# Setup of the S5 matrices and rotations, an early small tile, another order of the first loads, and where mixer pieces may stand in a one-core hybrid encoder layer

## The reference, cut to what matters

```
h = RMSNorm(x); u = h @ W_in          # four groups of heads
x += concat(RG-LRU, Mamba-2 SSD, gated DeltaNet, S5) @ W_out
x += CrossAttn(RMSNorm(x), memory)    # 4 heads, 256 memory tokens
x += SwiGLU(RMSNorm(x)); final RMSNorm
```

```
step = exp(log_dt);  mag = exp(a_re*step);  ang = a_im*step
lb = mag*(cos ang + i sin ang);  f = (lb - 1)/a
bb_re = f_re*b_re - f_im*b_im;   bb_im = f_re*b_im + f_im*b_re
s_t = lb*s_(t-1) + bb @ u_t;     y = Re(C s) + D u
```

## Time and profile before

| what | us |
|---|---|
| median of 3 runs | 4091.99 (4088.88 to 4100.78) |
| the profiled execution, its device time | 4092.89 |
| its span, first to last instruction | 4091.1 |
| TensorE busy | 3659.4 (89%) |
| VectorE busy | 2256.5 (55%) |
| ScalarE busy | 1335.2 (33%) |
| GpSimd busy | 126.5 (3%) |
| mean granted TensorE clock | 0.942 |

### The profile page before, as it was taken

One profiled execution on the slowest core, in us unless ns is written; L12 is line 12 of the kernel. 1 busy time (PEld: TensorE's weight loads), 2 busy tenths in 40 slices (PEclk: granted clock), 3 DMA queues, 4 the chain that ended last, 5 costly groups with the idle time before them and its releaser, 6 DMA issues.

```text
span 4091.1 us, 63447 instructions
## 1 busy us (share of the span) xinstructions
PE 3659.4 (89%) x24122; PEld 3547.7 (87%) x24122; DVE 2256.5 (55%) x4638; ACT 1335.2 (33%) x2474; POOL 126.5 (3%) x354
## 2 busy tenths in 40 slices
PE   6777868889798999998899998899998899999998
PEld 5766768889788999988899998899997899998998
DVE  6656744377674766573645573555564556553323
ACT  5443332254533333432322332323232322322101
POOL 2400000000000000000000000000000000000000
PEclk8977977799898999999999999999999999999999
DMA  6654476577767677768566668456667556567776
GB/s 216 228 180 155 164 237 224 168 237 269 250 221 276 232 251 265 269 209 281 180 210 208 231 218 282 171 189 226 222 226 255 191 188 210 198 210 253 248 252 218
DMA packets 371566, 912.03 MB, mean 223 GB/s; under 512 B 34752, under 2 KB 174528, under 8 KB 370752
## 3 DMA queue, kind: packets, MB, share of 16 engines
q1 hardware_dynamic: 371264, 907.99, 64.3%
HBM read 733.28 MB, written 174.57 MB: 222 GB/s over the span
## 4 chain that ended last, share of the span: by engine, by line
PE 50%; issue 20%; DVE 13%; DMA 5%; ACT 4%; DVEq 3%; POOLq 2%; SPq 1%; POOL 1%; ACTq 1%; PEld 0%; PEldq 0%
PE banks L461 14%; PE banks L463 13%; PE banks L462 13%; DMA wlo_sb<-kept_dram 2%; DVE wlo_sb L1121 2%; DVE uc_sb L1212 2%; PE banks L1611 1%; PE banks L1605 1%; DVE m_p_sb L2178 1%; PE banks L877 1%; PE banks L1614 1%; DMA kept_dram<-wlo_sb 1%; ACT whi_sb L929 1%; DMA ldb_sb<-y_dram 1%; DVE m_p_sb L2148 1%
## 5 line engine op out<-in xcount | busy, mean ns | idle before, releaser
L461 PE MATMUL banks<-hh_sb,whi_sb 128*128 128x384 f32 (+1 forms) x3360 | 1153.1, 343 | 117.2 <-DMA wlo_sb<-kept_dram 27.4
L462 PE MATMUL banks<-hh_sb,wlo_sb 128*128 128x384 f32 (+1 forms) x3360 | 1122.3, 334 | 0.0
L463 PE MATMUL banks<-hl_sb,whi_sb 128*128 128x384 f32 (+1 forms) x3360 | 1121.2, 334 | 0.0
L461 PEld LDWEIGHTS banks<-hh_sb,whi_sb 128*128 128x128 f32 x3360 | 652.7, 194 | 145.4 <-issue 46.4
L462 PEld LDWEIGHTS banks<-hh_sb,wlo_sb 128*128 128x128 f32 x3360 | 653.7, 195 | 1.4 <-issue 0.3
L463 PEld LDWEIGHTS banks<-hl_sb,whi_sb 128*128 128x128 f32 x3360 | 652.0, 194 | 0.0
L461 PE MATMUL banks<-g_hi_sb,whi_sb 128*128 128x384 f32 (+2 forms) x1504 | 514.5, 342 | 73.2 <-DVE x_sb L1317 26.8
L463 PE MATMUL banks<-g_lo_sb,whi_sb 128*128 128x384 f32 (+2 forms) x1504 | 501.3, 333 | 0.0
L462 PE MATMUL banks<-g_hi_sb,wlo_sb 128*128 128x384 f32 (+2 forms) x1504 | 501.2, 333 | 0.0
L461 PEld LDWEIGHTS banks<-g_hi_sb,whi_sb 128*128 128x128 f32 x1504 | 295.5, 196 | 87.5 <-DVE x_sb L1317 30.1
L1317 DVE TENSOR_TENSOR x_sb<-x_sb,banks 128x384 f32<-128x384 f32 (+2 forms) x400 | 202.4, 515 | 281.1 <-PE banks L463 272.1
(11 more groups left out here) (433 smaller groups left out, 5235.2 us busy)
## 6 DMA issues: line engine op xcount, KB each, us to landing
whi_sb<-kept_dram SPq DMA_DIRECT2D x504, 512.0 KB, 3.8
wlo_sb<-kept_dram SPq DMA_DIRECT2D x504, 512.0 KB, 4.9
raw_sb<-w SPq DMA_DIRECT2D x176, 512.0 KB, 5.3
kept_dram<-whi_sb SPq DMA_DIRECT2D x112, 512.0 KB, 5.5
kept_dram<-wlo_sb SPq DMA_DIRECT2D x112, 512.0 KB, 6.4
uc_dram<-uc_sb SPq DMA_DIRECT2D x90, 192.0 KB, 2.8
ldb_sb<-x_t SPq DMA_DIRECT2D x72, 192.0 KB, 4.7
plain_sb<-w SPq DMA_DIRECT2D x32, 256.0 KB, 4.8
```

What stands on the lines that cost most here:

```text
L461: eng.matmul(out, xh, yh, start=first, stop=False)
L462: eng.matmul(out, xl, yh, start=False, stop=False)
L463: return eng.matmul(out, xh, yl, start=False, stop=last)
```

## The change

It has six parts (the wait for `tail_loaded` is now in `dve_unit` for pass 0, the last two hunks are of `dve_mixer` and of ScalarE's block). `z0` becomes the third entry of stage A of pass 0, right after the first `st`, and the memory tiles are then prepared in `z0, u9, u10, u11`. `may_follow` also forbids pieces before a `pt`. `s5b` holds only the 16 columns of each matrix; GpSimd multiplies over 128 elements, clears bb (2 x 2 x 640) at its start and writes the blocks into it, and no longer computes `rot` but for its first column. The doubling steps run on VectorE at setup pieces 6 to 12; the first of them waits for `setup_pool` 5, and `setup_rot` tells their end. The token scalars of pass 0 are done earlier: ScalarE's part (`act_gates`) at setup piece 12, VectorE's reciprocal at 14. The first weight and three token tiles are loaded ahead of the constants, and ScalarE does one small activation before it waits for `par`.

```diff
     a = stage_a(0, h, n)
+    a[2:2] = [a.pop(-2)]
     h, n = new_h("M", 0), new_norm("M", 0)
     spread(a[2:6], preps("M", 0, h, n))
...
-    return not (... or i + 1 < len(SECS) and SECS[i + 1].kind == "st")
+    return not (... or i + 1 < len(SECS) and SECS[i + 1].kind in ("st", "pt"))
...
-            s5b = sb(st, "s5b", [P, 2, 1024])
-            bb = sb(st, "bb", [P, 2, 8, P])
+            s5b = sb(st, "s5b", [P, 2, 128])
+            bb = sb(st, "bb", [P, 2, 2, 640])
...
+            eng.wait_ge(tail_loaded, 16)
...
+        def sp_constants(eng):
+            eng.dma_start(stail[:]..., t["conv_caches"]).then_inc(tail_loaded, 16)
+            for name, dst in (("s5p", ...), ("s5b", ...), ("smix", smix[:]), ("mixc", mixc[:])):
+                eng.dma_start(dst, t[name]).then_inc(const_loaded, 16)
             if i == 0:
-                sp_weights(eng, 0, RAWS)
-                sp_tiles(eng, s.preps)
+                sp_weights(eng, 0, 1)
+                sp_tiles(eng, s.preps[:LDS])
+                sp_weights(eng, 1, RAWS)
+                sp_constants(eng)
+                sp_tiles(eng, s.preps[LDS:])
...
                 elif n == 12:
+                    act_gates(eng, 0)
...
+            eng.memset(bb[:], 0.0)
             eng.wait_ge(const_loaded, 16 * 4)
...
+            eng.tensor_copy(rot[:, 0, :, 0], w_cos)
+            eng.tensor_copy(rot[:, 1, :, 0], w_sin)
+            parts = [v3(bt[:, 0, j * 128:j * 128 + 128], 8) for j in range(4)]
+            for dst, f, b in zip(parts, (fr, fi, fr, fi), (b_re, b_im, b_im, b_re)):
+                tt(dst, f, b, ALU.mult)
+            eng.drain()
+            for part, op in ((0, ALU.subtract), (1, ALU.add)):
+                for half in range(2):
+                    r = slice(half * 64, half * 64 + 64)
+                    for j in range(2):
+                        at = slice(4 * j, 4 * j + 4)
+                        out = v3(bb[r, part, j, :], 4)[:, :, half * 16:half * 16 + 16]
+                        tt(out, parts[2 * part][r, at, :], parts[2 * part + 1][r, at, :], op)
             eng.drain().then_inc(setup_pool, 1)
...
+        def dve_rotations(eng, n):
+            cn = rot[:, 0, :, n - 1:n].unsqueeze(1).to_broadcast([P, 2, 8, n])
+            sn = sin[:, :, n - 1:n].to_broadcast([P, 8, n])
+            tt(ta, sin[:, :, 0:n], sn, ALU.mult)
+            tt(tb, cos[:, :, 0:n], sn, ALU.mult)
+            tt(rot[:, :, :, n:2 * n], rot[:, :, :, 0:n], cn, ALU.mult)
+            eng.drain()
+            tt(cos[:, :, n:2 * n], cos[:, :, n:2 * n], ta, ALU.subtract)
+            tt(sin[:, :, n:2 * n], sin[:, :, n:2 * n], tb, ALU.add)
+            eng.drain()
...
+                elif 6 <= n < 13:
+                    if n == 6:
+                        eng.wait_ge(setup_pool, 5)
+                    dve_rotations(eng, 1 << n - 6)
+                    if n == 12:
+                        eng.drain().then_inc(setup_rot, 1)
+                elif n == N_SETUP - 2:
+                    dve_invert(eng, 0)
...
             act.wait_ge(begun, 1)
+            act.activation(rms[:, 0:1], eps[:], ACT.Square)
             act.wait_ge(par_loaded, 16)
```

More of the change, by code:

```diff
@@ L356 @@
     SQ_COUNT.update((x.ni, x.sq + 1) for x in _s.preps if x.sq >= 0)
-Q_END = [max(s.q + s.nf for s in SECS if s.kind == "z" and s.p == p) for p in range(NP)]
+Q_END = [max(s.q + s.nf for s in SECS if s.kind in ("u", "z") and s.p == p) for p in range(NP)]
 Q_KV = max(s.q + 2 for s in SECS if s.kind in ("fs", "fv"))
@@ L400, in may_follow @@
     s = SECS[i]
-    return not (s.kind == "w" and s.a == KD - 1 or i + 1 < len(SECS) and SECS[i + 1].kind == "st")
+    return not (s.kind == "w" and s.a == KD - 1 or i + 1 < len(SECS) and SECS[i + 1].kind in ("st", "pt"))
 CHUNK_SECTIONS, SAMPLE_SECTIONS, SCALAR_SECTIONS, N_SETUP = 21, 25, 4, 16
@@ L1458, in after_mixer @@
             return bool(s.preps) and s.preps[0].kind == "Y"
+        def sp_constants(eng):
+            eng.dma_start(stail[:].rearrange("p a b c -> p (a b c)"), t["conv_caches"]).then_inc(tail_loaded, 16)
+            for name, dst in (("s5p", s5p[:].rearrange("p a b -> p (a b)")), ("s5b", s5b[:].rearrange("p a b -> p (a b)")),
+                              ("smix", smix[:]), ("mixc", mixc[:])):
+                eng.dma_start(dst, t[name]).then_inc(const_loaded, 16)
         def sp_section(eng, i):
@@ L1863, in pe_mixer @@
                         for s in range(8):
-                            last = eng.transpose(banks[:, 3 + 2 * part + s // 4, s % 4 * P:s % 4 * P + P],
-                                                 bb[:, part, s, :], ident)
+                            at = slice(s % 4 * P, s % 4 * P + P)
+                            last = eng.transpose(banks[:, 3 + 2 * part + s // 4, at], bb[:, part, s // 4, at], ident)
                     last.then_inc(setup_pe, 1)
@@ L2024, in act_scalars @@
             eng.drain().then_inc(tok_act, 1)
+        def act_scalars(eng, p):
+            n = tiles(p)
+            if p:
+                act_gates(eng, p)
             yield
@@ L2586, in setup @@
[L2586 to L2590, removed]
-            eng.drain()
[L2592 to L2604, removed]
-                tt(sin[:, :, n:2 * n], sin[:, :, n:2 * n], tb, ALU.add)
-                eng.drain()
-                if n > 1:
-                    yield
-                n *= 2
+            eng.tensor_copy(rot[:, 0, :, 0], w_cos)
@@ L2611, in dve_mixer, with dve_invert @@
+        def dve_invert(eng, p):
+            eng.wait_ge(tok_den, p + 1)
+            z = tk[:, 5, 0:tiles(p) * 8]
+            eng.reciprocal(z, z).then_inc(tok_inv, 1)
         def dve_mixer(eng):
@@ L2620, in dve_mixer @@
                 yield
-                eng.wait_ge(tok_den, p + 1)
-                z = tk[:, 5, 0:tiles(p) * 8]
-                eng.reciprocal(z, z).then_inc(tok_inv, 1)
+                if p:
+                    dve_invert(eng, p)
                 yield
@@ L2762, in _ @@
             dve.wait_ge(par_loaded, 16)
-            dve.wait_ge(tail_loaded, 16)
             weave(dve, dve_section, dve_mixer)
@@ L2774, in _ @@
             sp.dma_start(par[:], t["par"]).then_inc(par_loaded, 16)
-            sp.dma_start(stail[:].rearrange("p a b c -> p (a b c)"), t["conv_caches"]).then_inc(tail_loaded, 16)
-            for name, dst in (("s5p", s5p[:].rearrange("p a b -> p (a b)")), ("s5b", s5b[:].rearrange("p a b -> p (a b)")),
-                              ("mixc", mixc[:]), ("smix", smix[:])):
-                sp.dma_start(dst, t[name]).then_inc(const_loaded, 16)
             weave(sp, sp_section, sp_mixer)
```

32 lines of the change are left out of this document (15 added, 17 removed).

## The result

The changed kernel takes 4062.9 us (median of four runs, 4053.9 to 4067.9), the kernel before, on the same chip, 4096.4 (4088.9 to 4101.0). The ratio is 0.9921, with a 95% interval from 0.9908 to 0.9933: by the ratio 32 us off, where 48 were forecast. The profiled execution of the changed kernel is its fastest, 4053.93 us with a span of 4052.1: it ends 39 us earlier than the profiled execution of before. So the trace shows 7 us more than the medians, and I use it for where time went, not for how much in all.

A forecast was written before the change was run, and what follows sets the result against it. TensorE bounds the kernel from 1100 us on, so gains lie in the first 250 us and repeated gaps of later passes. Terms -6 - 4 - 13 - 5 - 20 = -48 take 4092.0 to 4044; range 4030 to 4058.

The forecast's parts named there:

- sign of being wrong: The prediction is wrong if the set-up and turn stretches are shorter and the passes as long as before.
- First loads: Kernel start: first weight and token tiles ahead of constants bring the first section forward; -6 us (3 to 9).
- z0 early: Set-up: `z0` moves from a stage bound by TensorE to one that is not; -4 us (0 to 7).
- Scalars early: Around `k13`: TensorE's 11.65 us wait for GpSimd's sums and the slow clock after it go; -13 us (8 to 15).
- Narrow matrices and rotations: Set-up, 103 to 172 us: GpSimd's interference goes (-17.5), VectorE gets doubling steps (+4) and a wait (+8); -5 us net.
- No mixer before a turn: Passes 1 to 4, `s1` to `s3`: stalls before turns go, part returns in `vo`; -20 us (5 to 40).
- Slower: Replanning: each of 110 displaced pieces lands where TensorE must wait, losing 60 us; 4104 us, chance 0.05.
- The turns gain nothing: Passes: the stall before the turn returns in `vo` because VectorE is behind there; 4064 us, chance 0.17.
- VectorE binds the setup: Set-up: the wait for GpSimd and all rotations are exposed, early `z0` brings nothing; 4061 us, chance 0.11.

The follow-up runs named there:

- z0s_late: Changed kernel with `z0` back before `z1`'s place and pass 0's token scalars back where they were; ratio to the kernel before 0.9945 (0.9929 to 0.9961).
- wide: Changed kernel with the 1024-column S5 matrices and the doubling steps back on GpSimd; ratio to the kernel before 0.9943 (0.9923 to 0.9963).
- rot_pool: Changed kernel, narrow matrices kept, with only the doubling steps back on GpSimd; ratio to the kernel before 0.9921 (0.9906 to 0.9936).
- turn_only: Kernel before with only the new rule of no mixer piece in front of a turn; ratio 0.9972 (0.9961 to 0.9983), 11.5 us faster.
- shift: Kernel before with mixer pieces from pass 0's windows on spread half a piece earlier, turns keeping theirs; ratio 1.0005 (0.9992 to 1.0019).
- hybrid: `rot_pool` with only pieces ahead of turns moved (into `s3`, `vo`) in passes 0, 1, 4, the change's spreading in 2, 3; 4043.0 us, ratio 0.9867.
- rp_late: `rot_pool` with the old plan, except places ahead of turns moved behind `vo` to free `g`, `up` or `so` sections; ratio 0.9945 (0.9928 to 0.9962).

## Why the prediction was right, and where it was off

Its signs came: the first product at 11.4 us, no wait of TensorE for GpSimd near 230, L1209's taps at 352 ns, VectorE's wait for GpSimd (8.1 us, 10 forecast), 20.6 us from `s1` to `s3` (but for pass 4) with waits ended by ScalarE's drain, new waits for L1317 (L1320 now) in `vo`. In passes 1 and 4 its sign of being wrong came as well: the stretches are shorter and the passes as long as before (-0.2 and +2.2 us). The direction and most mechanisms were right, and the sum was 16 us too large: by the ratios some 8 in the set-up and 8 at the turns. That it came out this near is in part luck, since in two terms errors of opposite sign cancel.

- **First loads, 6 us.** 5.4 at `u8` in this trace, 3.8 to 5.4 in all eight with these loads; in `z0s_late`, where no `z0` is in between, 4.6 are left at `k5`. Tile 3 was worked out to come at 15.8 us and came at 15.6. Right, and a little large.
- **z0 early, 4 us.** 1.2, not told from nothing. Against `z0s_late` it costs 1.5 us by `k0`, less than the 2.5 paid in the working, but 3.1 by `fs3.0`; and of the 6.9 us where it stood only 4.7 come free, since `fs3.1` then waits. The term took the removal for full, and nearly all is paid back.
- **Scalars early, 13 us.** The jump is 15 us, and 4.7 come back in `fv1`: 10.6. The step that failed is "what is late next is nothing that I find": it looked at chunk 0's loads, and the late one was ScalarE's work in chunk 0's first piece, behind a wait of 3.64 us for a weight.
- **Narrow matrices and rotations, 5 us net.** By the places at `k11`, 12.6 less 4.6 of loads and 1.2 of `z0`: 6.8, to some 2 us. The net was near by errors that cancel. I took the whole excess of VectorE (15.5 us) and 2 of clock as gain; the runs give some 9, since part of the excess lay beside ScalarE's work: where it is gone, VectorE waits longer for ScalarE before its splits (10.1 us before 14 splits in `wide`, 17.4 before 17 in `rot_pool`). And I charged 12 us for the wait and the steps on VectorE; they cost 3 to 6. The 8.1 us wait is real, but wait and steps together cost less than its length.
- **No mixer before a turn, 20 us.** The working was 55.5 gross, 15 for TensorE work that moves, 20 for stalls in `vo`. Passes 1 to 4 show 51.2 gross: 14.2, 15.0, 13.8 and 8.2, for pass 4 does not get to 20.6 but to 24.9. `vo` gives back 14.9 in the four (4.3, 4.4, 4.3, 1.9), of which 9.6 are longer busy time of TensorE, so that 5 are left for stalls, not 20. From `vo0.3` to `w7` of the next pass another 22.1 go (9.7, 3.4, 0.4, 8.6). So 37 us come back where 35 were charged, but mostly elsewhere: the total is near because the stalls in `vo` were priced some 15 us too high and the rest of the pass too low. What is left is 14 us in this trace, and 11.5 by the ratio of `turn_only`; of the difference to 20, some 4 are pass 4's stretch. The step that failed is the last: "110 pieces of five windows move by a section or so; I cost that at nothing, since their number is the same". 110 is the number of places that move. The pieces run in one order, so 273 of the 401 run later than before, by one to six sections, and their number is not the same in each part of a pass: the FFN's second half gets 25 pieces in place of 23, with 44 more products, some 5 to 8 us of TensorE in passes 1 and 2.

The rival *Slower* had this mechanism, with a price on each displaced piece. `shift` shows that being displaced costs nothing on the whole; the table shows that a placement has a price of its own in each of passes 1 to 4, of either sign. The rival *The turns gain nothing* is nearest to the total, 4064, and right in that `vo` gives part back, but the turns do keep more than half of what I gave them. *VectorE binds the setup* falls: from 103 to 172 us TensorE does more work than before, and wait and steps cost 3 to 6 us.

What stays open: which sections of the FFN make pass 4 dear and passes 2 and 3 cheap, whether `vo` would be free without any piece, and why pass 0 differs by up to 12 us between executions of one plan.

## What to carry to other kernels

Where side work is woven into a main stream by a spreading rule, a new exclusion re-deals every piece behind it. Write down which piece runs in which place before and after, and not only where the places are; price the new places section by section, and read the gain from one recurring point of a pass to the next, where from pass 1 on it repeats to 3 us while whole runs scatter by 10 and more. Here the first two pieces of a chunk in a row were 5 to 6 us dearer than with a section between them. When a stall is removed, follow the stretch behind it to the end of the pass: here some 37 of 51 us came back, part as moved work and part as stalls elsewhere. A helper engine's interference is worth less than the stretched time that it causes, because part of that lies beside other waits; and an expected wait costs less than its length for the same reason.

## What the hardware showed beyond that

- The stretching by GpSimd depends on the form of the instruction, more than I had used. VectorE by line in the kernel before, 103 to 172 us, a copy between two places of SBUF and an operation that reads a PSUM bank:

```profile
L1189 DVE COPY ust_sb<-stail_sb 128x24 f32<-128x24 f32 x4 | 3.0, 742 | 0.0
...
L1191 DVE TENSOR_TENSOR ust_sb<-banks,rstd_sb 128x128 f32<-128x128 f32 x4 | 1.1, 278 | 0.0
```

  The copy takes 173 ns in the changed kernel (L1192), the other 282 (L1194): a factor of four, and none. The section "Who interferes with whom" of SBUF — State Buffer in the Trainium skill says that an instruction with at most one SBUF input and outside the two-port modes doesn't contend, and that a copy can enter those modes; both rows agree.
- TensorE's clock in `vo`. The same 167 products from `s3` to `vo0.3` of pass 2 take 27.9 us at 0.94 of the clock in the changed kernel and 26.6 at 1.00, which is 2.4 GHz throughout, in `hybrid`. Both have one wait for VectorE's addition, of 2.2 and of 2.1 us. So after a wait of about this length the clock fell in one kernel and not in the other, and the 1.3 us between them go with it. In `rp_late`, with waits of 7.7 us, they take 34.3 at 0.90. A mean of 0.94 or 0.90 is some of the stretch at 1.2 GHz.
